# Plain fp32 down products, and expert rows scattered in two halves ahead of the next gather

## What is computed

```python
def swiglu(x, w_gate, w_up, w_down):
    return (jax.nn.silu(x @ w_gate) * (x @ w_up)) @ w_down

def moe_ffn(h, ...):          # 2112 tokens, 1024 wide; 64 experts of width 256, 8 per token
    idx, wts = ...            # the eight experts of each token and their weights
    routed = routed_experts(t, idx, wts, w_gate, w_up, w_down)   # sum of wts * swiglu(token, expert)
    shared = swiglu(t, w_sh_gate, w_sh_up, w_sh_down)            # one expert that all tokens pass
    return (routed + shared).reshape(shp)
```

## Time and profile before

| | us |
|---|---|
| median of two runs | 4903.41 (4898.7 to 4908.13) |
| the profiled execution, its own time | 4904.67 |
| its span | 4903.0 |
| PE busy | 4040.6 (82%) |
| DVE busy | 2481.5 (51%) |
| ACT busy | 1683.8 (34%) |
| POOL busy | 1164.0 (24%) |

### The profile page before, as it was taken

How to read it: one execution, slowest core, us unless ns; L and a number is a source line. 1 busy time by engine, 2 the same in 40 slices (tenths; PEclk the granted TensorE clock), 3 DMA queues, 4 the chain that set the end, 5 groups by cost and what they waited for, 6 DMA issues and landing times. The chain is left out here.

```text
span 4903.0 us, 69970 instructions
## 1 busy us (share of the span) xinstructions
PE 4040.6 (82%) x21435; PEld 2775.1 (57%) x21437; DVE 2481.5 (51%) x4223; ACT 1683.8 (34%) x3273; POOL 1164.0 (24%) x881
## 2 busy tenths in 40 slices
PE   6999989999888888688846788788888889898770
PEld 3444445555556666444425666676666677677650
DVE  1604965545555555355562265545545544544638
ACT  1001115445444444343312144334333333433420
POOL 0000000000033333200006644333333333333430
PEclk8999988768999999888868889899898999999985
DMA  3001320110099999821114277766766766766746
GB/s 96 17 26 64 107 91 1 35 36 9 12 363 393 390 406 372 337 69 60 59 38 162 83 215 222 219 179 167 210 166 189 209 167 150 208 153 170 232 106 209
DMA packets 324895, 784.15 MB, mean 160 GB/s; under 512 B 27560, under 2 KB 207144, under 8 KB 289382
## 3 DMA queue, kind: packets, MB, share of 16 engines
q0 software_dynamic: 95088, 470.92, 30.9%
q1 hardware_dynamic: 229630, 310.93, 19.0%
HBM read 642.81 MB, written 139.32 MB: 160 GB/s over the span
## 5 line engine op out<-in xcount | busy, mean ns | idle before, releaser
L1620 PE MATMUL gate_up_ps<-gu_high,x_highT 128*128 128x512 f32 x1416 | 617.7, 436 | 80.1 <-DVE x_lowT L1703 66.3
L1709 DVE TENSOR_TENSOR gu_low<-gu_raw,gu_high 128x1024 fp32r<-128x1024 f32 x260 | 541.6, 2140 | 211.7 <-ACT gu_high L1655 211.7
L200 PE MATMUL p_bank<-xT,wcol 128*128 128x512 f32 (+1 forms) x1600 | 593.3, 531 | 5.1 <-DMA wcol<-in_w_in_dram 3.3
L1621 PE MATMUL gate_up_ps<-gu_low,x_highT 128*128 128x512 f32 x1416 | 594.3, 420 | 0.0
L1622 PE MATMUL gate_up_ps<-gu_high,x_lowT 128*128 128x512 f32 x1416 | 591.5, 418 | 0.0
L200 PEld LDWEIGHTS p_bank<-xT,wcol 128*128 128x128 f32 x1600 | 278.6, 191 | 302.3 <-issue 300.8
L1730 DVE TENSOR_TENSOR hidden<-silu_gate,gate_up_ps 128x256 f32<-128x256 f32 x177 | 73.6, 416 | 628.2 <-ACT silu_gate L1680 628.2
L1535 POOL DMA_INDIRECT x_rows<-x_s,gather_now x179 | 174.8, 977 | 909.6 <-DVE gather_now L1697 877.4
L1620 PEld LDWEIGHTS gate_up_ps<-gu_high,x_highT 128*128 128x128 f32 x1416 | 294.4, 208 | 162.4 <-DVE x_lowT L1703 85.3
L559 PE MATMUL scores<-k_head,q_head 64*128 64x512 f32 (+3 forms) x640 | 349.5, 682 | 24.4 <-DMA v_head<-out_dram 20.8
L1543 POOL DMA_INDIRECT y_s<-y_rows,scatter_now x161 | 255.9, 1589 | 359.4 <-DVE y_rows L1721 300.7
(11 more groups left out here) (258 smaller groups left out, 6492.0 us busy)
## 6 DMA issues: line engine op xcount, KB each, us to landing
gu_raw<-in_w_gate_dram SPq DMA_DIRECT2D x64, 1024.0 KB, 5.7
gu_raw<-in_w_up_dram SPq DMA_DIRECT2D x64, 1024.0 KB, 12.0
down_raw<-in_w_down_dram SPq DMA_DIRECT2D x64, 1024.0 KB, 13.7
wcol<-in_w_in_dram SPq DMA_DIRECT2D x20, 512.0 KB, 4.0
x_s<-x SPq DMA_DIRECT2D x17, 512.0 KB, 2.6
xin<-in_x_prompt_dram SPq DMA_DIRECT2D x16, 512.0 KB, 3.6
out_dram<-rows POOLq DMA_DIRECT2D x8, 1024.0 KB, 8.3
x_res<-in_x_prompt_dram SPq DMA_DIRECT2D x16, 512.0 KB, 4.4
```

Source lines behind the costliest of these rows:

```text
L200: mm = nc.tensor.matmul(bank[c][:, 0:n], wcol[u][:, k, :], xT[:, k, s:s + n], start=(k == 0), stop=(k == KT - 1))
L1620: nc.tensor.matmul(out, x_high[:, k, :], both(gu_high, k), start=(k == 0), stop=False)
L1621: nc.tensor.matmul(out, x_high[:, k, :], both(gu_low, k), start=False, stop=False)
L1709: nc.vector.tensor_tensor(gu_low[u][:, at], raw_gu[u][:, at], gu_high[u][:, at], ALU.subtract).then_inc(gu_split, 1)
```

## The change

- The down weights are no longer split. SP loads them straight to `down`, one half of the buffer per expert, and PE uses them and the unsplit hidden rows `hT` in plain fp32: four products instead of twelve. ACT's cast of the down weights, POOL's `split_down` and DVE's `h_low` are gone.
- `g.y` becomes two scratch tensors of 512 columns, `y` two tiles, `to` two copies. The scatter of a block becomes two, of 128 rows of 2 KB each, with a completion semaphore of its own for each half. `combine` reads y with two transfers per tile, and the shared stage stores it with two.
- In POOL's order both scatters of a body come ahead of the gather.
- SP asks for the down weights of the next expert when the first body of the current one has done its down products (which frees that half of the buffer), and for gate and up behind that; before it was gate and up first, then down.
- PE's `begin` and `body` wait for the arrival of the down weights instead of their split.

The diff, cut to its core:

```diff
 (plan_dispatch)
-            pool.dma_start(g.y[SEQ:TP, :], nothing[0:TP - SEQ, :]).then_inc(table_out, 16)
-            pool.dma_start(g.y[TP:TRASH, :], nothing[0:TRASH - TP, :]).then_inc(table_out, 16)
+            for half in range(2):
+                pool.dma_start(g.y[half][SEQ:TP, :], nothing[0:TP - SEQ, 0:512]).then_inc(table_out, 16)
+                pool.dma_start(g.y[half][TP:TRASH, :], nothing[0:TRASH - TP, 0:512]).then_inc(table_out, 16)
 (experts, SP)
-                held(sp, d_split, e + 1, g.passed)
-                load_d(u, of(g.w_down, e + 1))
+                held(sp, downed, first * 2 + 2 * SH, g.passed)
+                load_d(1 - u, of(g.w_down, e))
 
             def store(n):
-                sp.wait_ge(y_act, n + 1)
-                sp.wait_ge(y_dve, n + 1)
-                sp.dma_start(g.y[ds(n * P, P), :], y[:]).then_inc(y_out, 16)
+                for half, kept in ((0, y_act), (1, y_dve)):
+                    sp.wait_ge(kept, n + 1)
+                    sp.dma_start(g.y[half][ds(n * P, P), :], y[half][:]).then_inc(y_out, 16)
...
+                    if gu_left or u:
+                        next_d(i * 2 + (2 - u), u, first)
+                    if gu_left - 1 + u > 0:
+                        next_gu(i * 2 + (2 - u), u)
 (experts, POOL)
-                held(pool, y_act, s + SH, g.passed)
-                held(pool, y_dve, s + SH, g.passed)
-                held(pool, to_ready, s + 1, g.passed)
-                pool.indirect_dma_start(out=g.y, out_offset=bass.IndirectOffsetOnAxis(ap=to[:], axis=0), in_=y[:],
-                                        in_offset=None, compute_op=ALU.add).then_inc(y_added, 16)
+                for half, kept in ((0, y_act), (1, y_dve)):
+                    held(pool, kept, s + SH, g.passed)
+                    held(pool, to_ready, s * 2 + (half + 1), g.passed)
+                    pool.indirect_dma_start(out=g.y[half],
+                                            out_offset=bass.IndirectOffsetOnAxis(ap=to[half][:], axis=0),
+                                            in_=y[half][:], in_offset=None, compute_op=ALU.add
+                                            ).then_inc(y_added[half], 16)
...
-                    split_down(i * 2 + (2 - u), u)
                     with pool.Fori(lower, upper) as m:
+                        scatter(m)
                         gather(m + (SH + 2))
-                        scatter(m)
 (experts, PE)
-                held(pe, h_low_kept, n + 1, g.passed)
+                held(pe, h_kept, n + 1, g.passed)
...
                 for half in range(2):
                     for k in range(F // P):
-                        nc.tensor.matmul(y_ps[half][:], h_high[:, k, :], down[:, w(HIGH, half, k)], start=(k == 0),
-                                         stop=False)
-                        nc.tensor.matmul(y_ps[half][:], h_high[:, k, :], down[:, w(LOW, half, k)], start=False,
-                                         stop=False)
-                        mm = nc.tensor.matmul(y_ps[half][:], h_low[:, k, :], down[:, w(HIGH, half, k)], start=False,
+                        mm = nc.tensor.matmul(y_ps[half][:], hT[:, k, :], down[:, w(half, k)], start=(k == 0),
                                               stop=(k == F // P - 1))
                     mm.then_inc(downed, 1)
...
-                    held(pe, d_split, own + e, g.passed)
+                    held(pe, d_in[u], own * 16 + (i * 16 + 16), g.passed)
 (experts, ACT, begin)
-                    act.wait_ge(gated, first + SH)
-                    held(act, downed, first * 2 + 2 * (SH - 1), g.passed)
-                act.wait_ge(d_in[u], (i + (1 if u or (isinstance(e, int) and e == 0) else 2)) * 16)
-                nc.scalar.copy(down[:, part(u, HIGH)], raw_d[u][:]).then_inc(d_cast, 1)
+                    held(act, gated, first + SH, g.passed)
 (experts, DVE)
-                    held(dve, y_added, m * 16, g.passed)
-                    nc.vector.tensor_copy(to[:], index[:, ds(n, 1), 0]).then_inc(to_ready, 1)
+                    for half in range(2):
+                        held(dve, y_added[half], m * 16, g.passed)
+                        nc.vector.tensor_copy(to[half][:], index[:, ds(n, 1), 0]).then_inc(to_ready, 1)
...
-                dve.wait_ge(h_high_kept, n + 1)
-                nc.vector.tensor_tensor(h_low[:], h_ps[:, 0:F].rearrange("p (k t) -> p k t", k=F // P), h_high[:],
-                                        ALU.subtract).then_inc(h_low_kept, 1)
 (combine, SP)
-                sp.dma_start(acc[u][0:n, :], g.y[at, :]).then_inc(tile_in[u], 16)
+                for half in range(2):
+                    sp.dma_start(acc[u][0:n, half * 512:(half + 1) * 512], g.y[half][at, :]).then_inc(tile_in[u], 16)
```

More of the change, by code:

```diff
@@ L1421, in experts @@
         index = sb("gather_index", [P, NBLK + 1, 2], U32)
-        now, to = sb("gather_now", [P, 1], U32), sb("scatter_now", [P, 1], U32)
+        now = sb("gather_now", [P, 1], U32)
+        to = [sb(f"scatter_now{half}", [P, 1], U32) for half in range(2)]
         GU, WD = 2 * 2 * D, 2 * D
         raw_gu = [sb(f"gu_raw{u}", [P, GU]) for u in range(2)]
-        raw_d = [sb(f"down_raw{u}", [P, WD]) for u in range(2)]
+        down = sb("down_w", [P, 2 * WD])
         gu_high = [sb(f"gu_high{u}", [P, GU], F32R) for u in range(2)]
         gu_low = [sb(f"gu_low{u}", [P, GU], F32R) for u in range(2)]
-        down = sb("down_parts", [P, 2 * 2 * WD], F32R)
-        HIGH, LOW = 0, WD
-        part = lambda u, which: slice(u * 2 * WD + which, u * 2 * WD + which + WD)
         xg = sb("x_rows", [P, D])
         x_high, x_low = sb("x_highT", [P, KT, P], F32R), sb("x_lowT", [P, KT, P], F32R)
-        h_high, h_low = sb("h_highT", [P, F // P, P], F32R), sb("h_lowT", [P, F // P, P], F32R)
-        sg, hid, y = sb("silu_gate", [P, F]), sb("hidden", [P, F]), sb("y_rows", [P, D])
+        hT = sb("hiddenT", [P, F // P, P])
+        sg, hid = sb("silu_gate", [P, F]), sb("hidden", [P, F])
+        y = [sb(f"y_rows{half}", [P, 512]) for half in range(2)]
         bank = lambda n: ctx.enter_context(nc.psum_tensor(n, [P, 512], F32))
@@ L1469, in pair @@
                     with eng.Fori(lower, upper) as m:
-                        body(m + SH, m, m > lower, i * 2 + (2 - u), u)
+                        body(m + SH, m, m > lower, i, u)
             with eng.Fori(0, E // 2 - 1) as i:
@@ L1518, in _, with pair @@
                 store(n)
-            with sp.Fori(0, E // 2 - 2) as i:
[L1520 to L1525, removed]
+            def pair(i, gu_left):
+                for u in (1, 0):
+                    _, (first,) = nc.values_load_multi_w_load_instructions(
+                        g.bounds[0:1, ds(i * 2 + (1 - u), 1)], (sp.engine,), min_val=0, max_val=MOST)
+                    if gu_left or u:
+                        next_d(i * 2 + (2 - u), u, first)
+                    if gu_left - 1 + u > 0:
+                        next_gu(i * 2 + (2 - u), u)
+            with sp.Fori(0, E // 2 - 2) as i:
+                pair(i, 2)
+            pair(E // 2 - 2, 1)
+            pair(E // 2 - 1, 0)
         @block.gpsimd
@@ L1583, in _ @@
             held(pool, x_arr, last * 16 + (16 * SH + 32), g.passed)
-            held(pool, y_added, last * 16 + 16, g.passed)
+            for half in range(2):
+                held(pool, y_added[half], last * 16 + 16, g.passed)
         @block.tensor
@@ L1597, in project, with body @@
             def project(n, at):
[L1599 removed]
+                held(pe, h_kept, n + 1, g.passed)
                 wait(pe, y_act, n)
                 held(pe, y_dve, n, g.passed)
[L1602 to L1604 removed]
+                w = lambda half, k: (slice(k * D + half * 512, k * D + half * 512 + 512) if isinstance(at, int) else
+                                     ds(at * WD + (k * D + half * 512), 512))
                 for half in range(2):
                     for k in range(F // P):
[L1607 to L1611 removed]
+                        mm = nc.tensor.matmul(y_ps[half][:], hT[:, k, :], down[:, w(half, k)], start=(k == 0),
                                               stop=(k == F // P - 1))
                     mm.then_inc(downed, 1)
[L1615 removed]
+            def body(n, m, own, i, u):
                 pe.wait_ge(xt_low, n * 2 + 2)
@@ L1638, in begin @@
                 held(pe, gu_split, e * PIECES + PIECES, g.passed)
+                if isinstance(e, int) and e == 0:
+                    pe.wait_ge(d_in[0], 16)
+                else:
+                    held(pe, d_in[1 - u], (i + (1 if u else 2)) * 16, g.passed)
             turn(0)
             blocks(pe, body, begin)
-            pe.wait_ge(d_split, E + 1)
+            pe.wait_ge(d_in[0], (E // 2 + 1) * 16)
             project(last_block(pe) + (SH - 1), 0)
@@ L1659, in keep_y @@
                 if m is None:
-                    wait(act, y_out, n * 16)
-                    nc.scalar.copy(y[:, 0:512], y_ps[0][:]).then_inc(y_act, 1)
-                else:
```

(13 more changed lines are left out.)

42 lines of the change are left out of this document (17 added, 25 removed).

## The result

The changed kernel takes **5912.56 us** (median of two runs, 5910.89 to 5914.23) against 4903.41 (4898.7 to 4908.13): a ratio of 1.206, 95% interval 1.202 to 1.210. The forecast was 5966, its range 5560 to 6260. The profiled execution has a span of 5912.3 us, and the mean granted clock fell from 0.88 to 0.831.

What follows compares the result with a forecast made beforehand. The prediction took a ring closing once per body through scatters, gather and TensorE's turn as the bound: 15.0 + 1.7 clock + 2.0 collisions = 18.7 us, times 160 = 2992 against 1931, 1061 more: 5966 us, range 5560 to 6260.

Steps and rivals of the forecast that it cites:

- the ring: Routed stage: down products, eviction, two scatters, gather and TensorE's next turn run one after another, 15.0 us a body.
- the clock: TensorE idling 5.0 us per body drops to the lower clock, slowing turn and products: 1.7 us a body, ends 0 and 4.3.
- the collisions: First bodies of an expert: weight loads and VectorE's split slow scatters and gather, 5.0 us per expert, 2.0 a body.
- What TensorE gets: Four plain down products replace twelve on TensorE: 3.52 us against 2.84, 0.68 us more per body.
- the gather stays hidden: Rival: the gather starts no later than 5.9 us after the turn, so only removals count: 4656 us, chance 3%.
- the first bodies' gain: Work taken from ScalarE, GpSimd and VectorE at an expert's first body: 5.6 us per expert, 358 us if nothing else moved.
- GpSimd by rows, not bytes: A half-row scatter takes GpSimd as long as a whole one, 1.59 us; by bytes it would be 0.8.
- The rival that went by bytes: GpSimd's scatter halves take 0.8 us and transfers stand 0.3 apart: 5085 us, or no change without clock and loads; chance 4%.
- The spacing between GpSimd's transfers: Gaps on GpSimd from half 0 to half 1 and from half 1 to the gather: 1.0 and 0.9 us.
- Queueing behind half 1: Half 1's bytes delaying the gather's landing: priced 0 to 1.3 us, taken as 0.
- The loads: Weight loads of 3 MB running under scatters and gather delay the gather's landing: 3.8 us per expert.
- VectorE's split beside GpSimd: VectorE's gate-up split slows half 1 and the gather on GpSimd: up to 2.2 us, taken as 1.2 per expert.

Runs made afterwards that it cites:

- the kernel with the gather ahead: The changed kernel with GpSimd's gather issued before the two scatters again, nothing else undone: 4600.12 us, ratio 0.939 to the kernel before.
- narrow scatters: The changed kernel with both scatters carrying 128 of 512 columns to scratch tensors that nothing reads, the rest of the routed result left out: 5751.48 us.

## Why the prediction was right, by its own steps

The mechanism stood in each step: the ring, the wait on every body, the clock, the collisions. Several sizes were off, and they cancelled. Means over 159 routed bodies of the changed kernel, beside the forecast's terms:

| part of the ring | forecast | measured |
|---|---|---|
| turn to index copy, with the clock's 1.7 | 6.51 | 6.87 |
| copy to half 0 | 1.00 | 1.05 |
| half 0 to half 1 | 2.59 | 1.88 |
| half 1 to the gather, with the split's 1.2 per expert | 2.97 | 2.17 |
| gather to turn, with the loads' 3.8 per expert | 5.62 | 6.49 |
| body | 18.7 | 18.46 |

- **What TensorE gets: right.** The forecast 0.68 us more for four plain products is 3.44 instead of 2.84, shown at full clock in the kernel with the gather ahead. Its rival "the gather stays hidden" was priced at 4656; made true by that kernel, it gives 4600. That the first bodies' gain would be worth nothing in the ring was right too.
- **GpSimd by rows, not bytes: right**, by 1.58 us for a half and 1.56 for a quarter of that. The rival that went by bytes falls.
- **The spacing between GpSimd's transfers: the step that failed in size.** It was 0.30 us on both places, where the prediction took 1.0 and 0.9 from the earlier trace rows. It read the 1.10 us there as the price of three satisfied waits. They were not satisfied. One row of before, beside the earlier trace rows, says so:

```profile
3339.89 0.73 DVE L1721 TENSOR_SCALAR y_rows<-y_ps,gather_index 128x512 f32<-128x512 f32 x1
```

  VectorE's half of `y` was done at 3340.62, after the gather's end at 3340.54, so the scatter was not one "for which all was ready". Its 1.10 us were a wait and the reaction to it, which "issue" does not name: in 153 of the 161 scatters of before, the start is 1.0 us behind the end of VectorE's half. Two places, 1.3 us a body too much: about 208 us.
- **Queueing behind half 1: priced at 0, of 0 to 1.3.** It was 5.58 against 4.10, so 1.48, just above the upper end. 1.0 of it goes with half 1's bytes, 0.25 with the 4.10, which was taken from the shared stage and is 4.36 for routed gathers of before; 0.2 stays open. The forecast lacked 237 us here. The estimate had compared when the last bytes of each land (14.8 and 15.0) and missed that half 1's bytes, under way at the same time, hold the gather's up even where they end first.
- **The loads: right in kind, too dear.** 3.8 us for each of 64 experts was taken from the earlier trace rows; it was 2.39 in 61 bodies. Among the loads the whole landing is the same 7.97 as there, so the 1.48 by which the other landings have grown don't come on top. By turns between two queues, which the Trainium skill states (DMA: Bandwidth & Descriptors, SWDGE vs HWDGE vs iDMA), the estimate was 1.5 us; the trace shows 2.39, more than that.
- **VectorE's split beside GpSimd: right in kind.** At an expert's begin, half 1 and the gather slow down, 1.58 to 2.56 and 1.01 to 1.41 us:

```profile
3563.15 1.58 POOL L1549 DMA_INDIRECT y_s<-y_rows,scatter_now  x1 [12.93 <-DVE scatter_now L1718]
...
3564.93 4.63 DVE L1706 TENSOR_TENSOR gu_low<-gu_raw,gu_high 128x1024 fp32r<-128x1024 f32 x4 [1.73 <-ACT gu_high L1656]
3565.03 2.56 POOL L1549 DMA_INDIRECT y_s<-y_rows,scatter_now  x1 [0.30 <-issue]
3567.90 1.41 POOL L1541 DMA_INDIRECT x_rows<-x_s,gather_now  x1 [0.30 <-issue]
```

  Over all bodies the step from half 1 to the gather is 2.17 us, and 1.87 without a split beside it: 0.30 a body, where the forecast had 0.48.
- **The clock: right, a little low.** 157 of 159 turns took 1.5 us or more, the lower of the two levels. Turn and products together take 1.75 + 4.62 = 6.37 us instead of 0.88 + 3.44 = 4.32: 2.05 against the forecast 1.7. The granted clock in the stretch of a turn and its products is 0.71, between the levels of 0.5 and 1 (in the row it stands behind PE, PEld, DVE, ACT and POOL), so it comes back within the products:

```profile
3518.40:3525.00 6.60, 6.60 (x19) 4.03 (x20) 1.41 (x3) 1.86 (x3) 0.00 (x0) 0.71 0.00 0
```

So 5966 came within 1% partly by luck: 1.3 us too much for the spacing, 0.6 too much for the loads and 0.2 for the split stand against 1.5 too little for the landing and 0.4 for the clock. Where the spacing alone had been read right, the forecast would have been about 5760, still inside the range.

## What to carry to other kernels

When an in-order engine both ends one iteration (a scatter of the result) and feeds the next (a gather), its order decides whether the iterations overlap: put first what the next iteration waits for, and look at each exchange of two calls as a possible ring through every engine. Shortening other work gains nothing once such a ring is closed (here about 300 us of gain turned into 1009 of loss), and the idling it makes costs a second time through the clock. Before a short gap in front of an instruction is read as overhead, look up when its last input was written.

## What the runs showed of the hardware that was not expected

- Three indirect transfers stand 0.30 us apart on GpSimd where nothing is waited for, with two semaphores to check (half 1) as with one (the gather).
- An accumulating scatter of 128 rows takes GpSimd 1.56 to 1.59 us for rows of 512 bytes, 2 KB and 4 KB alike; a gather 1.0. Both grow beside VectorE's split (2.56 and 1.41), which itself stays at 1.22 us a piece (at most 1.23).
- A gather of 512 KB lands 4.1 us after its start in the shared stage, 4.36 in the routed stage with the last scatter 4.6 us back or more, 4.56 behind narrow scatters, 5.58 with half a row's scatter started 1.9 us ahead or more, and 8.0 with that and 3 MB of weights on another queue. The first two of these growths are unexplained.
- Unused products that fill a wait made a kernel 209 us faster, by keeping the clock up for the products behind it. They are a test, not a cure: the order undone gives 1312.
